# The up product's result stores leave GpSimd's queue for ACT's, and the last unit's for SP's

## What is computed

```python
hid = jnp.square(jax.nn.relu(rmsnorm(x, g_pre_mlp) @ w_up))
x = x + rmsnorm(hid @ w_down, g_post_mlp)
```

## Time and profile before

| | |
|---|---|
| Time, median of three | 4103.48 us (4103.35 to 4111.6) |
| The profiled execution | 4099.91 us, its span 4098.1 us |
| Up product, first to last start of its matmuls | 2741.8 to 3385.2 us of the span |
| TensorE busy | 3601.6 us, 88% |
| ACT busy | 2204.4 us, 54% |
| GpSimd busy | 1042.6 us, 25% |
| Granted TensorE clock, mean | 0.934 |

### The profile page before, as it was taken

One profiled execution on the slowest core, in us unless ns is written; L12 is line 12 of the kernel. 1 busy time (PEld: TensorE's weight loads), 2 busy tenths in 40 slices (PEclk: granted clock), 3 DMA queues, 4 the chain that ended last, 5 costly groups with the idle time before them and its releaser, 6 DMA issues. The chain is left out here.

```text
span 4098.1 us, 52844 instructions
## 1 busy us (share of the span) xinstructions
PE 3601.6 (88%) x18061; PEld 2867.7 (70%) x18061; DVE 2866.0 (70%) x4922; ACT 2204.4 (54%) x3666; POOL 1042.6 (25%) x1120
## 2 busy tenths in 40 slices
PE   8999997778877479885499998989999998999998
PEld 7878776666755335544288886867888887888886
DVE  6685665887798889888778885666556554555565
ACT  3343323565677579987677774335455444443232
POOL 0000002554321011100156650115555551000011
PEclk9999998999977789997599999999999999999999
DMA  6555444334310044424346643567668656554464
GB/s 172 168 146 164 142 121 126 93 92 129 99 31 26 30 145 165 172 96 138 109 166 219 232 160 107 178 203 240 185 201 262 185 178 208 181 191 144 136 215 139
DMA packets 387598, 624.48 MB, mean 152 GB/s; under 512 B 97400, under 2 KB 216152, under 8 KB 379032
## 3 DMA queue, kind: packets, MB, share of 16 engines
q1 hardware_dynamic: 309560, 311.69, 25.6%
q0 software_dynamic: 77376, 309.63, 22.6%
q10 hardware_dynamic: 416, 0.02, 0.0%
HBM read 444.45 MB, written 176.77 MB: 152 GB/s over the span
## 5 line engine op out<-in xcount | busy, mean ns | idle before, releaser
L3731 PE MATMUL up_acc<-x_parts_first,w_up_parts 128*128 128x512 f32 x1536 | 361.4, 395 | 14.8 <-DVE w_up_parts L3484 14.8
L712 PE MATMUL accumulated<-hT,w_in_parts 128*128 128x512 f32 x1536 | 355.1, 391 | 0.0
L3731 PEld LDWEIGHTS up_acc<-x_parts_first,w_up_parts 128*128 128x128 f32 x1536 | 293.2, 191 | 77.3 <-DVE w_up_parts L3484 15.9
L2719 DVE TENSOR_SCALAR_CACHE_REDUCE junk_dve<-score,candidate 128x2048 bf16<-128x2048 f32 (+6 forms) x224 | 328.5, 1505 | 8.8 <-DVE candidate L2705 8.3
L712 PEld LDWEIGHTS accumulated<-hT,w_in_parts 128*128 128x128 f32 x1536 | 287.1, 188 | 60.2
L3822 PE MATMUL down_acc<-w_down_parts_even,hidden_parts 128*128 128x512 f32 x1344 | 315.7, 393 | 12.8 <-DVE hidden_parts L3520 10.1
L3822 PE MATMUL down_acc<-w_down_parts_odd,hidden_parts 128*128 128x512 f32 x1344 | 312.7, 390 | 0.0
L3822 PEld LDWEIGHTS down_acc<-w_down_parts_even,hidden_parts 128*128 128x128 f32 x1344 | 254.0, 189 | 67.2 <-issue 14.3
L2642 ACT ACTIVATE junk_act<-score,candidate 128x1920 bf16<-128x1920 f32 (+6 forms) x224 | 286.0, 1287 | 21.3 <-DVEq L2706 16.9
L3822 PEld LDWEIGHTS down_acc<-w_down_parts_odd,hidden_parts 128*128 128x128 f32 x1344 | 251.9, 188 | 53.2 <-issue 1.0
L3286 ACT ACTIVATE hidden_parts<-hidden_raw 128x1024 fp32r<-128x1024 f32 x112 | 118.7, 1059 | 310.8 <-PE down_acc L3822 289.0
(11 more groups left out here) (540 smaller groups left out, 8766.5 us busy)
## 6 DMA issues: line engine op xcount, KB each, us to landing
hidden_raw<-scratch_hs POOLq DMA_DIRECT2D x112, 512.0 KB, 4.5
w_in_raw<-in_w_in SPq DMA_DIRECT2D x80, 512.0 KB, 4.0
up_raw<-scratch_ws SPq DMA_DIRECT2D x128, 256.0 KB, 2.9
scratch_hs<-hidden_even POOLq DMA_DIRECT2D x112, 256.0 KB, 5.0
scratch_hs<-hidden_odd POOLq DMA_DIRECT2D x112, 256.0 KB, 4.8
up_raw<-in_w_up SPq DMA_DIRECT2D x96, 256.0 KB, 5.6
weight_sums<-in_w_down POOLq DMA_DIRECT2D x16, 1024.0 KB, 5.3
scratch_wt<-weight_sums POOLq DMA_DIRECT2D x16, 1024.0 KB, 5.4
```

Of the source, the lines that this page charges most:

```text
L712: mm = pe.matmul(z, w2[:, g % 2, b, k2 * ST + n * P:k2 * ST + (n + 1) * P], h[:, a, k, :], start=(first and j == 0), stop=(last and j == 2))
L2719: dve.tensor_scalar(jd[:, n % 2, 0:WIDTH[i]], score[:, SOFF[i]:SOFF[i + 1]], cf[:, c:c + 1], None, ALU.is_ge, ALU.add, accum_out=cnt[:, c: ...
L3731: mm = pe.matmul(up_bank(n), wp[:, n % SLOTS, b, q * P:(q + 1) * P], X(i)[:, a, q, :], start=(q == 0 and (a, b) == (0, 0)), stop=(q == QUA ...
```

## The change

`store_hidden` for units 0 to 30 is issued by ACT, one unit later: within unit u + 1, at its product P7. The last unit's is issued by SP, after its loads for the turn and before b piece 8. GpSimd keeps the sums and loses all 224 store issues. What is stored, from where and to where, is the same.

```diff
@@ SP
+                def store_hidden(u):
+                    h, f = UNITS[u]
+                    sp.wait_ge(hid_rdy, 4 * u + 4)
+                    sp.wait_ge(hsum_rdy, 4 * u + 4)
+                    for i in range(NPROD):
+                        sp.dma_start(sc["hs"][i, 4 * h:4 * h + 4, :, f, :].rearrange("r p t -> p r t"),
+                                     H(u)[:, i, :].rearrange("p (r t) -> p r t", r=4)).then_inc(hs_out[u % 2], 16)
...
                 sp.dma_start(fold[:, :], io["fold"][:, 0:SR]).then_inc(const_in, 16)
+                store_hidden(NU - 1)
                 loaded_w = S_RAW
@@ GpSimd
-                def store_hidden(u):
...
                     hidden_sums(u)
-                    store_hidden(u)
@@ ACT
+                def store_hidden(u):
+                    h, f = UNITS[u]
+                    act.wait_ge(hid_rdy, 4 * u + 4)
+                    act.wait_ge(hsum_rdy, 4 * u + 4)
+                    for i in range(NPROD):
+                        act.dma_start(sc["hs"][i, 4 * h:4 * h + 4, :, f, :].rearrange("r p t -> p r t"),
+                                     H(u)[:, i, :].rearrange("p (r t) -> p r t", r=4)).then_inc(hs_out[u % 2], 16)
...
                     if n >= 0 and n % NPROD in (P6, P3, P4):
                         square_hidden(n // NPROD, (P6, P3, P4).index(n % NPROD))
+                    if n >= NPROD and n % NPROD == P7:
+                        store_hidden(n // NPROD - 1)
                     if n == LAST_UP - 3:
                         b_high(0)
                         b_high(1)
```

## The result

The changed kernel takes 4113.01 us (median of 11 runs, 4105.47 to 4116.93); the kernel before, run beside it, 4103.35 us (11 runs). The ratio of the two is 1.0018, with a 95% interval of 1.0010 to 1.0026: slower by 7.4 us (4.1 to 10.7). The two medians lie further apart, 9.7 us; the ratio is the one to go by. It is just inside the 0.2% (8.2 us) that the prediction called the same, and its interval reaches past it. The profiled execution took 4105.47 us, the shortest of the 11, with a span of 4103.7 us; the span of before was 4098.1 us.

A forecast was written before the change was run, and what follows sets the result against it. TensorE was taken to bound the steady units, so only the second half's first unit and the turn could move; 0 + 1 + 5.0 = +6.0 us gave 4109.5 us against the median of the runs, range 4100 to 4119.

The forecast's parts named there:

- the forecast's own range: Whole kernel: 4102 to 4113 us, the range without the rivals; the forecast had a chance of 0.55.
- rival C: Second half's first unit: ACT's issues take 1 us and more each, +10 to +13 with the turn, 4113 to 4117; chance 0.22.
- one of the prediction's own signs of being wrong: On ACT: the prediction is wrong if ACT's store issues block for over a microsecond each.
- The steady unit, nothing: Steady up-product units: seven ACT issues take 3.4 to 7 us within 9.6 us free, so they cost nothing.
- Rival D: Every unit: ACT becomes the bound from 1.37 us an issue, up to 4204 us; chance 0.06.
- The second half's first unit, +1: Where ACT splits the second half's x: ACT comes 1 to 6 us later, TensorE waits +1 us, bounds -2.6 to +5.
- The turn, +5.0: Up to down product: b piece 8 lands late behind SP's seven stores, delaying step 2; +5.0 us, bounds -2.2 to +7.6.
- The turn-taking of packets: At the turn: DMA engines alternate queues packet by packet, so GpSimd's loads go first and piece 8 takes 14.4 us.
- the lower bound of 7.0 us: At the turn: piece 8 lands 7.0 us after SP's first store if it waits for its own queue alone.
- Rival B: The turn gets shorter: piece 8 lands within 8 us of the first store, at most 5.2 us gained; chance 0.17.

The follow-up runs named there:

- changed again: The changed kernel measured and profiled a second time, with no edit: 4110.54 us, ratio 1.0023 to the kernel before.
- the first pair of experiments: Changed kernel with the last unit's stores back on GpSimd, ratio 1.0008; kernel before with only the last unit's stores on SP, ratio 1.0014.
- half by GpSimd: The changed kernel with the stores of units 14 and 15 issued by GpSimd again: 4106.13 us, ratio 1.0015 to the kernel before.

## Why the prediction held, and where its terms were off

The forecast of 4109.5 us (4100 to 4119, same 0.64, slower 0.33) holds: 4113.01 us, and a ratio just within 0.2%. On which side of that line it fell was luck: the second measurement of the same kernel gives 1.0023, which is beyond it. Both places that it named are the places that moved. Its sum of +6.0 us stands against +7.4 and +9.4 us measured. 4113.01 is also the upper end of the forecast's own range and the lower end of rival C's, and at the second half it is C's condition that came true: one of the prediction's own signs of being wrong, issues of over a microsecond each, was seen there (1.5 us in the mean) and not in the steady units (0.85).

**The steady unit, nothing.** Right. Seven issues took 5.97 us, in the range of 3.4 to 7, TensorE 256.00 of 256 us. The kernel in which ACT stores 29 units away from the two disputed places gives 0.9998. Rival D, ACT as the bound, wants 1.37 us an issue; the median was 0.84.

**The second half's first unit, +1.** This is the mis-sized term: it measured +5.3 and +5.5 us, just past the upper bound of +5. Its step that failed is "as most of the issues should be of the median kind". It took the row of four short runs a partition at 0.51 us, and the store's own median is 0.82 to 0.84 us and its mean here 10.3/7 = 1.5 us; 10.3 us lie beyond the 3.4 to 8 that it allowed. What ACT gets back was under-counted too: 1.4 to 2.7 us were allowed, from two of four waits on loads, and all 4.3 us went. The two misses offset in part, and the 3.9 us by which ACT is late lie within the forecast's 1 to 6. Rival C gave the mechanism: issues of over a microsecond where SP's loads fill the engines (share 0.91). The stores on ACT in these two units alone make it, and without them it is gone. Of the 5.3 us, TensorE's waits are 5.86 - 2.60 = 3.3, which the bound of +5 covers. Most of the rest is the clock: behind the wait of 4.69 us the records show the lower level,

```profile
3095.00:3099.00 4.00, 3.93 (x9) 3.14 (x10) 4.00 (x8) 0.35 (x1) 0.00 (x0) 0.50 0.75 222
```

a granted clock of 0.50, 1.2 GHz, and the 24 matmuls took 7.71 us, 1.7 more than before. The prediction had no term for that here. It did allow for a clock that falls at the turn, where it cancels.

**The turn, +5.0.** The chain behind SP's first store went as written. Piece 8 was to land 13.0 us after that store and landed 12.1 us after (3407.59 + 4.41 = 3412.0); step 2 was to follow 4.2 us after that and followed after 4.0. Between the first store and step 2 lie 16.1 us, and 16.0 in changed again (3403.3 to 3419.3), against 17.2 forecast. `load_a(3)` behind the same stores was the right row to go by.

That step 2 was forecast at 3416.1 and came at 3416.01 is luck. The last 24 up matmuls start 2.8 us later in this trace than before (3382.78 against 3380.02), and the forecast has them at the old place. Counted from them, the first store was forecast at 18.9 us and came at 17.1 (18.8 in changed again), and step 2 at 36.1 and came at 33.2 (34.8).

What the prediction had no term for is ACT's own issuing at the turn. It let the sums end 1.2 us sooner than before, from what GpSimd's queue does alone; but in the chain of the changed kernel ACT's issues of unit 30's stores stand ahead of them. From the start of the last 24 up matmuls the sums took 20.1 us before, 17.0 after and 18.7 in changed again, so they were 3.0 and 1.3 us sooner, and ACT's issues end at 3.3 and 5.6 us (the table under the first pair of experiments). By the measure of the forecast (from those matmuls to the second half of step 3, 41.8 us before) the turn took 44.4 and 46.8 us: prices of 2.6 and 5.0. The 5.0 is even with the forecast by two misses that offset: step 2 came 1.2 us early, and from there to the second half of step 3 it took 12.0 us in place of 10.7. The prediction let the slow matmuls behind the idle time cancel; half a step took 4.48 us before, 4.93 after and 5.46 in changed again.

The turn-taking of packets, by which the price would be that of 14.4 us, was not far off: 12.1 us, with the hardware queues' packets still small (56.92 MB in 114992 packets, 495 bytes each, on ACT's). The rule of the Trainium skill (DMA: Bandwidth & Descriptors, "Queues, rings and completion order") was nearer than the lower bound of 7.0 us from SP's queue alone. That does not show the rule at work: no run here separates the turns from the issuing, which by itself took 7.7 of the 12.1 us.

**Rival B, a turn that gets shorter.** It did not come, but what it saw is real and larger than it said. With three loads moved ahead of the stores, the way to step 8 is 7.6 to 9.8 us shorter than before. Its gain of 5.2 us lay behind the order on SP. The Trainium skill (the same page, "Issuing engines are not separate DMA queues") says that starting DMAs from several engines saves only the sequencer's time, usually small. As a forecast of this change, 5.2 us won and none lost at the turn, it is not borne out: the turn lost 2.6 to 5.2 us. What that rule leaves out is who stands behind the engine that issues and waits; the order of SP's program alone moves step 8 by 12.4 us, with the same bytes over the same 16 engines.

**Open.** Why the start scatters over 8.6 us between executions and kernels whose code there is the same; with that, why half by GpSimd is not faster by time as its parts are. Why seven issues took 10.3 us at the second half and 5.97 in a steady unit was only argued from the DMA share: no run issued them there with the loads held back. A rival is that the issues of SP and ACT hold each other. SP's loads are slow there too, up to 1.67 us before (where GpSimd stored, at an even 0.75 each) and 1.18 after, where most take 0.32; no run separates the two.

## What to carry to other kernels

Before an engine or a queue gets a store that waits, list what its program has next and who stands behind that. The three loads issued ahead of SP's wait turned 2.6 to 5.2 us lost into 7.6 to 9.8 us won. A store moved onto a compute engine costs its issues in the place with the least slack, not on average: price it there by the dearest issues of the trace, and add the lower clock behind a wait that it makes. Look for such places at changes of stage, and let those few units keep the old engine. And count a forecast's times from the last point that the change leaves alone: a time on the clock can agree while its parts do not.

## What the runs showed of the hardware

Issuing is not a fixed cost. Stores of the same shape from ACT took 0.37 to 3.23 us each. In a steady unit the first three of the seven took 0.37, 0.54 and 0.64 us and the later four 0.88 to 1.23; at the second half it went up from the third on, and the sixth took 3.23 us. On SP they took 0.38 to 1.94. GpSimd took 5.2 to 5.3 us for the same seven in every place looked at.

The same stores are cut in different packets by the two kinds of queue. q0 lost 17920 packets and 58.7 MB (the earlier trace rows and the page after), 3278 bytes each; q10 has 114992 for 56.92 MB, 495 bytes each. The DMA share of the steady stretch rose from 0.62 to 0.69 at nearly the same GB/s (190 and 194).

What the 24 matmuls behind a wait cost does not follow from its length alone. At the second half they took 6.02 to 6.07 us behind waits of 1.66 to 2.60 us (five traces), 7.36 and 7.38 us behind 2.77 and 3.13, and 7.71 to 8.52 us behind 4.66 to 4.69 (five traces). But at the first unit, where TensorE had stood 3.0 to 3.7 us one product earlier, the same 24 matmuls took 7.09 to 7.35 us behind waits of 2.29 to 2.81 us in all twelve traces.
